# Cached values of a two-layer hybrid decoder: probabilities held stationary, pages moved, four batches in four column groups

## The chip, the cores and the metric

The kernel runs on one core of one Trainium2 chip. The metric is device time in microseconds (us) of one execution, as a median of several.

## The reference, cut to what matters

Two decoder layers run over 520 tokens: one prompt of 512, and a sample group of 8 sequences with one new token each. Each sample sequence has 1024 past tokens in a paged cache, eight pages of 128, and a page table that says which. The part of the mixer on which the change works:

```python
def gather_past(pool, page_table):
    g = pool[page_table]
    return g.reshape((g.shape[0], g.shape[1] * g.shape[2]) + g.shape[3:])
...
(a_q, a_k, a_v, a_iq, a_ik, a_iw, b_q, b_k, b_v, ..., gate) = jnp.split(xn @ w['w_in'], offs, axis=-1)
# A, sparse attention: 4 query heads, 2 key/value heads, top 256 keys by an indexer
p = jax.nn.softmax(logits, axis=-1)
o = jnp.einsum('btjgn,btnjd->btjgd', p, v_sel)
# B, stick-breaking attention, 4 heads
a = jnp.where(mask, jnp.exp(jax.nn.log_sigmoid(z) + after), 0.0)
o = jnp.einsum('bhtl,blhd->bthd', a, v)
...
g = jax.nn.sigmoid(gate.reshape(bsz, t, N_BRANCH, D_MODEL))
merged = g[:, :, 0] * (o_a @ w['w_br_a']) + ... + g[:, :, 3] * (o_d @ w['w_br_d'])
```

A page of cached values holds 384 numbers for each of its 128 tokens: 128 of A (two heads of 64) and 256 of B (four heads of 64). The other two branches are scans over the prompt in chunks of 128 (C, a matrix memory with a norm, and D, a state-space model), four heads each. The gate logits are 4096 columns of the input projection, that is 32 weight tiles of 128 columns. After the mixer come an output projection and a convolutional feed-forward part.

## The kernel before

**Order of a layer.** Weights are loaded as tiles of 128 partitions by 1024 columns. A layer has 29 projection tiles (12, then the cached keys, then 17), 32 gate tiles, then the branch, output, up and down tiles. TensorE, VectorE (DVE), ScalarE (ACT), GpSimd (POOL) and SyncE (SP) each run one program in a fixed written order; semaphores tie them together. A wait such as `pe.wait_ge(*sa_trc.nth(l, 0))` names a signal and the layer.

**Ring and queue.** SP issues nearly all loads, in the order of the list `TILES`. They go into the ring `R` of four slots; a load into a slot waits for `tile_used`, the count of tiles that TensorE is done with. A page of the cache needs its number from the page table `PT` first (`value_load`, line 403), then its own DMA (line 404). SP also stores the gate logits, two halves per tile, with `keep` (line 447).

**Split weights.** A projection or gate tile is multiplied as three matmuls per pass: leading parts `XH` and `WH`, rests `XL` and `WL`. ACT makes `WH` (line 1003, `split`), for the gate tiles POOL makes `WL` (line 1714, `split_rest`). There are two buffers of each, so tile q+2 is split when tile q has been multiplied.

**Gate filling.** The 32 gate tiles are used as filling between other work. The generator `gates(l)` (line 582) yields after each unit of three matmuls of 260 columns; a tile has 16 units, and `fill(upto)` on TensorE runs units until `upto` are done. ACT's `drain(upto)` copies finished halves out of the banks (line 1021) and starts the split of tile q+2; POOL's `follow(upto)` starts the rest. Tables say how far each place fills: `PRE` (seven places before the scans), `LOOP` (eight scan steps), `IN_T` (four places in each of the four attention blocks).

**Places around the change.** After the last projection come, in this order: the transposing of A's sample probabilities (lines 680 and 682); 12 transposes to token-major, `TO_TM` (line 695), each a chunk of four; cumulative sums of the gate logarithms (line 706) and a transpose of rows; the sample group's recurrent state in eight diagonals of 8 rows, which POOL builds and TensorE broadcasts; then eight scan steps v (0 to 3 for C, 4 to 7 for D); then four attention blocks t of the prompt. In a scan step TensorE broadcasts a row (line 758), makes scores (line 776), multiplies cached values, and runs the numerator (line 779); ACT makes decays (line 1166), POOL a diagonal mask (line 1708) and state weights (line 1770), DVE products. After steps 1 and 3 DVE divides (line 1585).

**Cached values.** The probabilities of all sample batches stand in `PA`, a view of `QB`: 256 columns of A, then 256 of B, 32 for each page position. `cached_values(l, b)` (lines 557 and 562) is called once per scan step, for one of the eight batches. Each of its pages is held stationary in three pieces of 128 columns, and the moving operand is 4 columns of probabilities for A, and 2 for each pair of heads of B:

```python
mm(PS[:, 7, 448 + 4 * b:448 + 4 * b + 4], slot(l, n)[:, v0:v0 + 128],
   PA[:, 32 * j + 4 * b:32 * j + 4 * b + 4], start=j == 0, stop=j == 7, ...)
```

These are 192 matmuls a layer, in full fp32 precision. The result is already laid out by feature; nine DVE operations after the scans add it to `OS` and copy it to the branch inputs (signal `sa_out`), for which TensorE waits in the first attention block. The pages lie in the same ring as the gate tiles, interleaved by the list `MIX`: four slots of two pages for each batch.

## Time and profile before

| | |
|---|---|
| median of 3 runs | 2830.28 us (2822.64 to 2831.82) |
| the profiled execution: its time, its span | 2841.91 us, 2839.8 us |
| its mean granted TensorE clock | 0.895 |
| TensorE busy with matmuls | 2540.2 us, 89% |
| DVE, ACT, POOL busy | 1285.4, 1013.4, 348.1 us |
| TensorE's share of the chain that ended last | 31%, DVE 4%, ACT 1% |
| matmuls of gate filling (line 582) | 3072, about 900 us |

A busy TensorE need not be at full speed: the granted clock tells how fast it ran, as a share of 2.4 GHz, and 0.5 is the lower of its two levels. Matmuls overlap each other, so that busy times of single matmuls add up to more than the time they span. The other engines have much slack on average, so what they cost is seen only where TensorE waits for them. The name PEld is the weight load of TensorE, and SPq and ACTq are DMAs issued by SyncE and ScalarE.

### The profile page before, as it was taken

To read this page: it belongs to the slowest core of one execution; us is meant where nothing else is said; L and a number is where in the kernel's file an instruction comes from. 1 tells how busy PE (TensorE), PEld (TensorE's weight loads), DVE (VectorE), ACT (ScalarE), POOL (GpSimd) and SP (SyncE) were. 2 spreads that over 40 slices of the span, in tenths; PEclk is the share of its full clock that TensorE was granted. 3 is DMA by queue.
4 is the path that set the end of the run, shared out by engine and by line. 5 is a ranking of instruction groups with operands and counts; after the bars stand their busy time and mean duration, and the time that the engine had idled before them with its cause. 6 is when DMAs were issued, how large, how long until landed. Compare 5 with 4: busy or idle time off the path is not lost. (4 is left out here: it accounts for less than half of the span.)

```text
span 2839.8 us, 41630 instructions
## 1 busy us (share of the span) xinstructions
PE 2540.2 (89%) x16456; PEld 2175.6 (77%) x16456; DVE 1285.4 (45%) x2047; ACT 1013.4 (36%) x1526; POOL 348.1 (12%) x390
## 2 busy tenths in 40 slices
PE   6999679989999889999888997899899997999996
PEld 5659657767887789999885686477687776999895
DVE  3329341223556465662342383422234565666623
ACT  3123431224444345552230225222244433555521
POOL 0014232112320000000000132311222100000000
PEclk9999766769999899999999997676799998999998
DMA  3362112232326122222314422122322251222221
GB/s 151 111 201 90 58 47 77 77 100 68 89 75 196 60 67 91 97 91 82 103 60 148 156 75 68 58 68 83 92 79 89 84 172 52 83 97 90 88 84 60
DMA packets 111827, 264.00 MB, mean 93 GB/s; under 512 B 13458, under 2 KB 47250, under 8 KB 110738
## 3 DMA queue, kind: packets, MB, share of 16 engines
q1 hardware_dynamic: 99074, 238.25, 26.4%
q10 hardware_dynamic: 12560, 23.11, 2.4%
q8 instruction: 130, 2.13, 0.3%
q14 instruction: 63, 0.52, 0.1%
HBM read 233.71 MB, written 27.59 MB: 92 GB/s over the span
## 5 line engine op out<-in xcount | busy, mean ns | idle before, releaser
L497 PE MATMUL PS<-XH,WH 128*128 128x260 f32 x2592 | 540.2, 290 | 47.9 <-DVE XL L1315 36.3
L1003 ACT ACTIVATE WH<-R 128x1024 fp32r<-128x1024 f32 x270 | 286.0, 1059 | 780.5 <-PE PS L497 564.9
L497 PE MATMUL PS<-XL,WH 128*128 128x260 f32 x2592 | 529.2, 286 | 4.3 <-issue 2.8
L497 PE MATMUL PS<-XH,WL 128*128 128x260 f32 x2592 | 528.1, 285 | 0.0
L1339 DVE TENSOR_TENSOR WL<-R,WH 128x1024 fp32r<-128x1024 f32 x176 | 215.7, 1226 | 555.9 <-ACT WH L1003 555.6
L497 PEld LDWEIGHTS PS<-XH,WH 128*128 128x128 f32 x2592 | 408.6, 193 | 56.7 <-issue 43.7
L497 PEld LDWEIGHTS PS<-XL,WH 128*128 128x128 f32 x2592 | 406.3, 192 | 4.7 <-issue 4.7
L497 PEld LDWEIGHTS PS<-XH,WL 128*128 128x128 f32 x2592 | 405.7, 192 | 0.0
L582 PE MATMUL PS<-XH,WH 128*128 128x260 f32 x1024 | 304.8, 298 | 16.5 <-ACT RB L1021 16.3
L1714 POOL TENSOR_TENSOR WL<-R,WH 128x1024 fp32r<-128x1024 f32 x94 | 223.3, 2376 | 730.8 <-ACT WH L1003 729.9
L582 PE MATMUL PS<-XL,WH 128*128 128x260 f32 x1024 | 298.3, 291 | 0.0
L582 PE MATMUL PS<-XH,WL 128*128 128x260 f32 x1024 | 297.0, 290 | 0.0
L582 PEld LDWEIGHTS PS<-XH,WH 128*128 128x128 f32 x1024 | 202.4, 198 | 29.9 <-issue 22.2
L582 PEld LDWEIGHTS PS<-XH,WL 128*128 128x128 f32 x1024 | 202.1, 197 | 0.0
L582 PEld LDWEIGHTS PS<-XL,WH 128*128 128x128 f32 x1024 | 202.0, 197 | 0.0
L497 PE MATMUL PS<-FR,WH 128*128 128x260 f32 x1024 | 190.8, 289 | 8.9 <-issue 8.9
L497 PEld LDWEIGHTS PS<-FR,WH 128*128 128x128 f32 x1024 | 154.4, 195 | 9.7 <-issue 9.7
L1318 DVE SCALAR_TENSOR_TENSOR S<-S,V 128x510 f32<-128x510 f32 (+1 forms) x176 | 132.1, 751 | 44.9 <-ACT S L1282 41.8
L1021 ACT ACTIVATE RB<-PS 128x260 f32<-128x260 f32 x128 | 49.6, 387 | 246.8 <-PE PS L582 144.7
L915 PE MATMUL PS<-F,R 128*128 128x260 f32 x512 | 119.4, 388 | 4.5 <-DVE F L1315 3.1
L915 PEld LDWEIGHTS PS<-F,R 128*128 128x128 f32 x512 | 94.4, 190 | 29.1 <-DVE F L1315 9.8
L562 PE MATMUL PS<-QB,R 128*128 128x2 f32 x512 | 113.0, 325 | 0.0
(311 smaller groups left out, 3398.9 us busy)
## 6 DMA issues: line engine op xcount, KB each, us to landing
R<-w_up SPq DMA_DIRECT2D x88, 512.0 KB, 3.3
R<-w_gate SPq DMA_DIRECT2D x64, 512.0 KB, 3.7
R<-w_proj SPq DMA_DIRECT2D x58, 512.0 KB, 3.3
R<-v_c SPq DMA_DIRECT2D x128, 192.0 KB, 2.4
R<-w_down SPq DMA_DIRECT2D x44, 512.0 KB, 3.2
R<-k_c SPq DMA_DIRECT2D x72, 256.0 KB, 3.3
GATES<-RB SPq DMA_DIRECT2D x128, 130.0 KB, 3.7
S<-GATES SPq DMA_DIRECT2D x64, 260.0 KB, 2.7
```

The lines of the kernel that those rows point to most:

```text
L497: i = mm(PS[:, bank + a, 0:HALF], p[:, w, k * 128:(k + 1) * 128], x[:, a * HALF:(a + 1) * HALF], start=first and p is WH and x is hi, stop ...
L562: ins = mm(PS[:, 7, o:o + 2], slot(l, n)[:, v0 + 128 + 128 * c:v0 + 256 + 128 * c], PA[:, 256 + 32 * j + 4 * b + 2 * c:256 + 32 * j + 4 * ...
L582: i = mm(PS[:, 1 + 2 * a, 0:HALF], p[:, half(l, m), k * 128:(k + 1) * 128], x[:, k, a * HALF:(a + 1) * HALF], start=k == 0 and p is WH and ...
L915: ins = mm(PS[:, 4 + 2 * (q % 2) + a, 0:HALF], slot(l, nb)[:, 256 * br + 128 * k:256 * br + 128 * k + 128], F[:, o + k, a * HALF:(a + 1) * ...
L1003: do(A(WH[:, half(l, m), :], slot(l, SPLIT[m]), ACT.Copy), w_hi)
L1021: do(A(RB[:, HALF * a:HALF * (a + 1)], PS[:, 1 + 2 * a, 0:HALF], ACT.Copy), g_out)
L1318: do(v_.scalar_tensor_tensor(out, a, sc, b, o0, o1), s)
L1339: v_.tensor_tensor(WL[:, half(l, m), :], slot(l, SPLIT[m]), WH[:, half(l, m), :].bitcast(f32), ALU.subtract).then_inc(w_lo.sem, 1)
L1714: g_.tensor_tensor(WL[:, half(l, m), :], slot(l, SPLIT[m]), WH[:, half(l, m), :].bitcast(f32), ALU.subtract).then_inc(w_lo_p.sem, 1)
```

## The change

**Cached values.** Now 8 columns of probabilities are stationary, A's four and B's four of one batch side by side (`PA` is now a view with 8 columns for each batch and page position), and a whole page of 384 columns moves. Four batches are multiplied in one call, a quad: their results go to partitions 0, 32, 64 and 96 of one bank, which are four column groups of TensorE. A layer has 16 quads of four matmuls, eight for the first four batches (bank 0) and eight for the last four (bank 2). As every matmul adds to its bank (`start=False`), one matmul of 384 columns with zeros clears each bank first. A finished bank is copied by ACT (`values_out`) and turned to feature-major by three small matmuls (`by_feature`).

**Buffers.** The pages have left the ring. Two buffers of four pages each, `QUAD`, lie in parts of `S` and `TM` that are free at that time. Each page is still its own DMA with its number from `PT`, all on SP, four for each quad; quad k waits until quad k-2 has been used.

**Place.** Quads 0 and 1 stand before the token-major transposes, and two more follow each of the first seven chunks. The DVE operations, 18 instead of nine since each half is done apart, move in front of the state products, and TensorE waits for them before `r_tr`, not in the attention blocks.

**Filling.** The tables are new: 144 units up to the end of the token-major transposes where there were 48; 192 before the diagonals (96), four after each of the eight diagonals, eight after each scan step (16 after every second one), and 10 to 26 at each place of the attention blocks instead of 12 to 42. After the last scan step 288 units are done where it was 160. Tile q+2 is always split as soon as tile q is finished, by ACT in `drain` and by POOL in `follow`; the loop `IN_LOOP`, by which both split the next tile in a scan step ahead of the filling, is gone.

**ACT.** The exponential of A's sample probabilities stands after the last projection copy instead of inside the loop over them, and TensorE waits for the last two projection copies before it fills.

```diff
...
-PRE = [0, 32, 48, 64, 72, 80, 96]
-LOOP = [96 + STEPS * (v // 2 + 1) for v in range(8)]
...
+LAST, PAST_P = 16, 24
+IN_TM = [36, 48, 60, 72, 84, 96, 108, 112, 120, 128, 136, 144]
+CUM, ROWS, SEL, DOTS = 160, 176, 184, 192
+IN_R = [DOTS + 4 * (s + 1) for s in range(8)]
+LOOP = [IN_R[-1] + 8 * (v + 1) for v in range(8)]
+IN_T = [[14, 10, 12, 10], [14, 10, 18, 12], [14, 10, 22, 14], [14, 10, 26, 14]]
...
+QUADS_AT = [PAST_P, PAST_P] + [IN_TM[i] for i in range(7) for _ in range(2)]
+LOAD_QUADS = [[k for k in range(NQ) if (QUADS_AT[k - 2] // STEPS + RING - 1 if k >= 2 else 1) == q] for q in range(NG)]
...
@@ sync engine
+                def cached_values(k):
+
+                    s, j = divmod(k, PAGES)
+                    if k == 0:
+                        sp.wait_ge(*sb_a.nth(l, 0))
+                    elif k >= 2:
+                        sp.wait_ge(*quad_used.nth(l, k - 2))
+                    for g in range(4):
+                        sp.dma_start(QUAD[k % 2][:, g, :],
+                                     v_c[l, bass.ds(page(sp, PAGES * (4 * s + g) + j), 1)].rearrange("o p c -> (o p) c")
+                                     ).then_inc(quad_full[k % 2].sem, 16)
+                for q in range(NG):
+                    tile(l, AT["gate", q], w_gate[l, q], 1024)
+                    if q >= RING:
+                        keep(q - RING)
+                    for k in LOAD_QUADS[q]:
+                        cached_values(k)
...
@@ tensor engine
+            def cached_values(l, k):
+
+                s, j = divmod(k, PAGES)
+                pe.wait_ge(quad_full[k % 2].sem, 64 * (NQ // 2 * l + k // 2 + 1))
+                for g in range(4):
+                    ins = mm(PS[32 * g:32 * g + 8, 2 * s, 0:V_REC], PA[:, PAGES * j + 4 * s + g, :], QUAD[k % 2][:, g, :],
+                             start=False, stop=j == PAGES - 1, skip_group_check=True)
+                finish(ins, quad_used)
...
+                for c in (NPROJ - 2, NPROJ - 1):
+                    pe.wait_ge(*proj_out.nth(l, c))
+                fill(LAST)
...
+                for s in range(2):
+                    mm(PS[:, 2 * s, 0:V_REC], K[0:1, C_SEL + 128:C_SEL + 256], K[0:1, 0:V_REC], start=True, stop=False,
+                       skip_group_check=True)
+                fill(PAST_P)
                 pe.wait_ge(*sa_trc.nth(l, 0))
                 pe.wait_ge(*sa_own.nth(l, 0))
+                cached_values(l, 0)
+                cached_values(l, 1)
...
+                    fill(IN_TM[i])
+                    if i < 7:
+                        cached_values(l, 2 * i + 2)
+                        cached_values(l, 2 * i + 3)
+                    if i in (4, 9):
+                        by_feature(l, i // 5)
...
                     finish(ins, r_bc)
+                    fill(IN_R[s])
...
@@ scalar engine
-                        if a:
-                            for nxt in SPLIT_NEXT[q]:
-                                split(l, NPROJ + nxt)
+                        if a and q + 2 < NG:
+                            split(l, NPROJ + q + 2)
...
-                    for q in IN_LOOP[v]:
-                        split(l, NPROJ + q)
...
@@ gpsimd engine
+                    follow(IN_R[s])
...
-                    for q in IN_LOOP[v]:
-                        split_rest(l, NPROJ + q)
                     follow(LOOP[v])
```

Three places of the resulting order follow. In the rows, L is the line, xN a repetition, and the names in brackets are signals waited for.

SP, the start of the gate tiles, in the kernel before (`w_gate` is a gate tile, `GATES` the store of two halves, `v_c` a page of cached values with the table read of `PT` ahead of it):

```order
L424 DMA R<-w_gate 128x1024 [waits tile_used] x5
L447 DMA GATES<-RB 128x260 [waits gate_logits_copied] x2
L424 DMA R<-w_gate 128x1024 [waits tile_used]
L447 DMA GATES<-RB 128x260 [waits gate_logits_copied] x2
L403 TENSOR_LOAD PT [waits tile_used]
L403 ISA x2
L404 ISA
L404 DMA R<-v_c 128x384
...
L404 DMA R<-v_c 128x384
L447 DMA GATES<-RB 128x260 [waits gate_logits_copied] x2
L403 TENSOR_LOAD PT [waits tile_used]
```

The same place after:

```order
L433 DMA R<-w_gate 128x1024 [waits tile_used] x2
L405 TENSOR_LOAD PT [waits sample_b_weights]
L405 ISA x2
L465 ISA
L465 DMA S<-v_c 128x384
...
L465 DMA TM<-v_c 128x384
L433 DMA R<-w_gate 128x1024 [waits tile_used] x3
L454 DMA GATES<-RB 128x260 [waits gate_logits_copied] x2
L405 TENSOR_LOAD PT [waits value_pages_used]
L405 ISA x2
L465 ISA
L465 DMA S<-v_c 128x384
```

The pages came after six gate tiles, and between each two of them stood stores of gate halves. Now the first eight stand after two tiles, the next ones after three more, and eight pages, of two quads, stand between neighbouring tiles or groups of tiles.

TensorE, between the last projection and the first gate filling, before (680 and 682 transpose the probabilities, 695 is the token-major transpose of `F`, 582 the gate filling):

```order
L680 MATMUL PS<-K,S 128x32 [waits sample_a_probs]
L680 MATMUL PS<-K,S 128x32 x7
L682 MATMUL PS<-DG,K 128x32
L695 MATMUL PS<-K,F 128x128 [waits rope_done,projection_copied,sample_a_own_value,sample_a_probs_copied]
L695 MATMUL PS<-K,F 128x128 x3
L695 MATMUL PS<-K,F 128x128 [waits projection_copied]
L695 MATMUL PS<-K,F 128x128 x3
...
L695 MATMUL PS<-K,F 128x128 [waits projection_copied,token_major_ready]
L695 MATMUL PS<-K,F 128x128 x3
L582 MATMUL PS<-XH,WH 128x260 [waits weight_rest_part_ready_by_pool,weight_leading_part_ready]
L582 MATMUL PS<-XL,WH 128x260
```

The same place after (702 and 704 answer to 680 and 682, 707 is the clearing of the banks, 601 the filling, 570 a quad, 723 the token-major transpose):

```order
L702 MATMUL PS<-K,S 128x32 [waits sample_a_probs]
L702 MATMUL PS<-K,S 128x32 x7
L704 MATMUL PS<-DG,K 128x32
L707 MATMUL PS<-K 128x384 x2
L601 MATMUL PS<-XH,WH 128x260 [waits gate_logits_copied,weight_rest_part_ready_by_pool,weight_leading_part_ready]
...
L570 MATMUL PS<-S,QB 8x384 [waits value_pages0_loaded,sample_a_own_value,sample_a_probs_copied]
L570 MATMUL PS<-S,QB 8x384 x3
L570 MATMUL PS<-TM,QB 8x384 [waits value_pages1_loaded]
L570 MATMUL PS<-TM,QB 8x384 x3
L723 MATMUL PS<-K,F 128x128 [waits projection_copied,rope_done]
L723 MATMUL PS<-K,F 128x128 x3
L601 MATMUL PS<-XH,WH 128x260 [waits gate_logits_copied]
```

Before, eight chunks of transposes followed each other without filling; now two quads stand ahead of the first chunk, and 12 units and two quads behind it.

ACT, scan steps 1 and 2, before (1164 and 1166 are the decays, 1003 the split of a gate tile, 1021 the copy of a half, 1177 and 1179 the norm of C):

```order
L1166 ACTIVATE F<-F 128x1280 [waits decay_exponent_ready]
L1003 ACTIVATE WH<-R 128x1024 [waits tile_used,slot3_full,decay_exp_done]
L1021 ACTIVATE RB<-PS 128x260 [waits gate_half0_stored,gate_first_half_done,weight_leading_part_ready]
L1021 ACTIVATE RB<-PS 128x260 [waits gate_half1_stored,tile_used,gate_logits_copied]
L1164 ACTIVATE F<-PS,SMT 128x512 [waits numerator_done,row_broadcast,gate_logits_copied]
...
L1166 ACTIVATE F<-F 128x1280 [waits decay_exponent_ready]
L1177 ACTIVATE S<-PS 128x512 [waits numerator_done,decay_exp_done]
L1179 ACTIVATE S<-S 128x520 [waits c_h_ready,c_denominator_abs]
```

The same place after (1201 and 1203 are the decays, 1031 the split, 1049 the copy, 1212 and 1214 the norm):

```order
L1203 ACTIVATE F<-F 128x1280 [waits decay_exponent_ready]
L1049 ACTIVATE RB<-PS 128x260 [waits gate_half0_stored,gate_first_half_done,decay_exp_done]
L1201 ACTIVATE F<-PS,SMT 128x512 [waits numerator_done,row_broadcast,gate_logits_copied]
...
L1203 ACTIVATE F<-F 128x1280 [waits decay_exponent_ready]
L1212 ACTIVATE S<-PS 128x512 [waits numerator_done,decay_exp_done]
L1214 ACTIVATE S<-S 128x520 [waits c_h_ready,c_denominator_abs]
L1049 ACTIVATE RB<-PS 128x260 [waits gate_half1_stored,tile_used,c_squares_ready]
L1031 ACTIVATE WH<-R 128x1024 [waits tile_used,slot1_full,gate_logits_copied]
L1201 ACTIVATE F<-PS,SMT 128x512 [waits numerator_done,row_broadcast,weight_leading_part_ready]
```

The split stood ahead of both copies, and the step's decays behind them; now it stands behind the second copy, which itself has moved behind the norm of C.

## Rows read from the trace of the kernel before

**Rows 1.** Page, part 1: busy time, share of the span, instructions.

```profile
PE 2540.2 (89%) x16456; PEld 2175.6 (77%) x16456; DVE 1285.4 (45%) x2047; ACT 1013.4 (36%) x1526; POOL 348.1 (12%) x390
```

**Rows 2.** Windows, layer 0: length, busy PE, PEld, DVE, ACT, POOL; PEclk; DMA share; GB/s.

```profile
302.70:351.60 48.90, 28.70 (x204) 27.13 (x203) 19.14 (x45) 30.48 (x50) 9.47 (x4) 0.82 0.22 73
351.60:407.40 55.80, 45.98 (x212) 31.68 (x212) 29.12 (x51) 15.53 (x26) 18.84 (x13) 0.74 0.17 55
407.40:611.10 203.70, 191.41 (x860) 142.43 (x860) 39.33 (x58) 47.25 (x67) 43.44 (x102) 0.68 0.27 81
611.10:857.60 246.50, 226.17 (x1425) 185.68 (x1425) 114.59 (x280) 105.57 (x189) 57.95 (x56) 0.93 0.27 79
```

**Rows 3.** Windows, PE, probabilities' tile only, scans of both layers.

```profile
sum 420.00, PE 143.22; mean PE 71.61
```

**Rows 4.** Timeline, PE: start, us, instruction, count, [idle before]; first and last pages.

```profile
421.44 0.59 PE L557 MATMUL PS<-QB,R 128*128 128x4 f32 x2
...
422.74 0.57 PE L557 MATMUL PS<-QB,R 128*128 128x4 f32 x2
...
449.12 0.39 PE L557 MATMUL PS<-QB,R 128*128 128x4 f32 x2
...
449.81 0.36 PE L557 MATMUL PS<-QB,R 128*128 128x4 f32 x2
```

**Rows 5.** Windows, PE, line 582 only: length, busy, clock, DMA; 16 units each.

```profile
353.20:361.50 8.30, 8.22 (x48) 0.69 0.00 0
439.50:445.60 6.10, 6.04 (x48) 1.00 0.00 0
```

**Rows 6.** Timeline, PE, cached keys of layer 0.

```profile
144.26 0.61 PE L637 MATMUL PS<-R,QI 64*32 64x256 f32 x2
144.80 0.40 PE L639 MATMUL PS<-R,QA 128*32 128x256 f32 x1
144.81 0.40 PE L647 MATMUL PS<-R,QB 128*32 128x256 f32 x1
...
145.79 0.62 PE L637 MATMUL PS<-R,QI 64*32 64x256 f32 x2
```

**Rows 7.** Timeline, SP, layer 0; last line: page, part 6.

```profile
342.74 1.45 SPq L404 DMA_DIRECT2D R<-v_c  x2
344.23 0.91 SPq L447 DMA_DIRECT2D GATES<-RB  x2
...
R<-v_c SPq DMA_DIRECT2D x128, 192.0 KB, 2.4
```

**Rows 8.** Timeline, splits, POOL's weights and DVE's reciprocal, scans of layer 0.

```profile
452.07 1.37 POOL L1708 TENSOR_SCALAR_AFFINE_SELECT F<-F 128x128 f32<-128x128 f32 x4 [16.04 <-ACT F L1166]
...
454.52 2.05 POOL L1770 TENSOR_SCALAR S<-TM,U 128x64 f32<-128x64 f32 x4
...
468.39 3.35 DVE L1585 RECIPROCAL S<-S 128x512 f32<-128x512 f32 x1
...
581.88 1.06 ACT L1003 ACTIVATE WH<-R 128x1024 fp32r<-128x1024 f32 x1 [1.91 <-DMA R<-w_gate]
...
583.08 2.35 POOL L1714 TENSOR_TENSOR WL<-R,WH 128x1024 fp32r<-128x1024 f32 x1 [14.15 <-ACT WH L1003]
```

**Rows 9.** Waits, PE, whole kernel: waited for, total us, times, longest.

```profile
PE PS L706 <- DVE SMT L1315: 17.4, 2, 8.7
```

**Rows 10.** Timeline, ACT, sigmoid and SiLU ahead of the scans, layer 0.

```profile
384.10 1.28 ACT L1153 ACT_TABLE_LOAD   x1
...
388.01 1.30 ACT L1155 ACTIVATE F<-F 128x520 f32<-128x520 f32 x2
```

**Rows 11.** Timeline, last attention block of layer 0.

```profile
802.43 1.84 ACT L1208 ACTIVATE F<-PS 128x512 f32<-128x512 f32 x4 [1.56 <-PE PS L849]
...
810.57 1.37 POOL L1708 TENSOR_SCALAR_AFFINE_SELECT F<-F 128x128 f32<-128x128 f32 x4 [8.17 <-DVE F L1318]
...
838.59 0.15 DVE L1321 TENSOR_SCALAR MX<-MX 128x1 f32<-128x1 f32 x1
```

More of the change, by code:

```diff
@@ L214, in trunk_kernel @@
         slot_full = [sig(f"slot{i}_full", 0) for i in range(RING)]
-        tile_used = sig("tile_used", NPROJ + 2 * NU + 40 + 8 + 44 + 22)
+        tile_used = sig("tile_used", NPROJ + NU + 40 + 8 + 44 + 22)
+        quad_full = [sig(f"value_pages{i}_loaded", 0) for i in range(2)]
+        quad_used = sig("value_pages_used", NQ)
         xt_ready = sig("normalised_ready", 16)
@@ L436, in _ @@
                     if not by_act(u):
-                        cached(sp, l, AT["K", u], u, K_REC, k_c)
+                        cached_keys(sp, l, u)
                 for c in range(CUT, NPROJ):
                     tile(l, proj(c), w_proj[l, c], 1024)
-                def keep(n):
-                    if TILES[n][0] == "gate":
-                        q = TILES[n][1]
-                        for a in range(2):
-                            sp.wait_ge(*g_out.nth(l, 2 * q + a))
-                            sp.dma_start(GATES[l, q, :, HALF * a:HALF * (a + 1)],
-                                         RB[:, HALF * a:HALF * (a + 1)]).then_inc(g_stored[a].sem, 16)
@@ L449, in _, with keep @@
-                for kind, i in MIX:
-                    n = AT[kind, i]
-                    if kind == "V":
-                        cached(sp, l, n, i, V_REC, v_c)
-                    else:
-                        tile(l, n, w_gate[l, i], 1024)
-                    keep(n - RING)
+                def keep(q):
+                    for a in range(2):
+                        sp.wait_ge(*g_out.nth(l, 2 * q + a))
+                        sp.dma_start(GATES[l, q, :, HALF * a:HALF * (a + 1)],
+                                     RB[:, HALF * a:HALF * (a + 1)]).then_inc(g_stored[a].sem, 16)
@@ L456, in _ @@
+                for q in range(NG):
[4 more added lines that the diff above has]
+                        cached_values(k)
                 for d in range(2):
                     tile(l, AT["br", d], w_br[l, d], 1024)
-                    keep(AT["br", d] - RING)
-                for n in range(AT["br", 2] - RING, AT["br", 0]):
-                    keep(n)
+                for q in range(NG - RING, NG):
+                    keep(q)
@@ L709, in _ @@
                 finish(ins, sm_cum)
-                fill(PRE[3])
+                fill(CUM)
                 pe.wait_ge(*sm_rt.nth(l, 0))
@@ L714, in _ @@
                 finish(ins, sm_tr)
-                fill(PRE[4])
+                fill(ROWS)
                 pe.wait_ge(*xbc_ready.nth(l, 5))
@@ L722, in _ @@
                 finish(ins, r_sel)
-                fill(PRE[5])
+                fill(SEL)
                 pe.wait_ge(*r_prod.nth(l, 0))
@@ L730, in _ @@
                 finish(ins, r_tr)
-                fill(PRE[6])
+                fill(DOTS)
                 for s in range(8):
@@ L1049, in _ @@
                             if by_act(u):
-                                cached(act, l, AT["K", u], u, K_REC, k_c)
+                                cached_keys(act, l, u)
                         split(l, CUT)
@@ L1109, in _ @@
                     token_major(c)
-                token_major(7)
-                drain(PRE[1])
-                for i in range(8, len(TO_TM)):
+                for i in range(7, len(TO_TM)):
                     token_major(i)
-                drain(PRE[2])
                 act.wait_ge(*sm_v.nth(l, 0))
@@ L1149, in _ @@
                 do(A(S[0:8, 3, 0:512], PS[0:8, 2, :], ACT.Copy), r_trc)
-                drain(PRE[6])
+                drain(DOTS)
+                for s in range(8):
+                    drain(IN_R[s])
                 for c in range(2):
@@ L1492, in _ @@
                 tt(MR, SROW[0:4, :], PS[64:68, 5, :], ALU.add, sm_g)
+                for s in range(2):
+                    dve.wait_ge(*sv_out.nth(l, s))
+                    o = OS[:, 16 * s:16 * s + 16]
+                    tt(o, o, PS[:, 2 * s, 384:400], ALU.add)
+                    for h in range(4):
+                        r0 = 64 * (h // 2)
+                        do(v_.tensor_copy(F[r0:r0 + 64, AQ + h % 2, NPR + 4 * s:NPR + 4 * s + 4], o[r0:r0 + 64, h:16:4]))
+                    for h in range(4):
+                        r0, c = 64 * (h % 2), h // 2
+                        do(v_.tensor_copy(F[r0:r0 + 64, BQ + c, NPR + 4 * s:NPR + 4 * s + 4],
+                                          PS[r0:r0 + 64, 2 * s, 400 + 8 * c + h % 2:408 + 8 * c:2]),
+                           sa_out if s and h == 3 else dve_own)
                 dve.wait_ge(*tm_ready.nth(l, 9))
@@ L1733, in follow @@
                     while STEPS * (behind[0] + 1) <= upto:
-                        for nxt in SPLIT_NEXT[behind[0]]:
-                            split_rest(l, NPROJ + nxt)
+                        if behind[0] + 2 < NG:
+                            split_rest(l, NPROJ + behind[0] + 2)
                         behind[0] += 1
-                follow(PRE[4])
+                follow(DOTS)
                 pool.wait_ge(*r_trc.nth(l, 0))
```

111 lines of the change are left out of this document (48 added, 63 removed).

## The prediction

> **What bounds the kernel now.** I read the page's table of engines, then the busy time by stage, then each engine's instructions inside the stages. TensorE is busy 89% of the span [rows 1], so what counts is its own work, its waits and its clock. In layer 0 the touched stretch runs from 302.7 to 857.6 us, and I call its four parts turn, rows, scans and attention: 48.9, 55.8, 203.7 and 246.5 us, with granted clocks of 0.82, 0.74, 0.68 and 0.93 of 2.4 GHz [rows 2]. Layer 1 has the same four parts shifted by about 1407 us (the matmuls of the cached values take 143.22 us in the two windows, 71.6 in each) [rows 3], so I work out one layer and double it. The 71.4 us of layer 0's cached values lie wholly in the scans and wholly on TensorE's path. A page (three matmuls, six passes) takes 1.30 us at the start of one batch and 0.69 us at the start of another [rows 4], a factor of nearly two: these matmuls move 2 or 4 columns each, and the clock falls to 1.2 GHz while they run. A gate tile is 16 units; 16 units take 6.04 us at clock 1.00 and 8.22 us after a long wait at 0.69 [rows 5]. So a unit is 0.375 us, and a long wait costs about 2.2 us more in lost clock.
>
> **Turn, +59.8 us a layer.** It holds 144 units where it held 48. The start: gate halves share banks with the last two projections, so TensorE waits for ACT's split and copy, 1.06 us [rows 8] and an estimated 0.8; 16 units 6.0; transposed probabilities 0.8 and the two zeroing matmuls 1.3 (estimates from passes, below); 8 units 3.0. That is 13.0. Then seven steps of one chunk transposed, 12 units and two quads. **The quads on TensorE:** the change has 64 matmuls of 384 moving columns a layer. Cached keys show the nearest row: fp32 matmuls of 256 columns start a pass every 0.24 us, and two in neighbouring column groups start 0.01 us apart, so that eight passes take 1.53 us instead of about 1.9 [rows 6]. By columns a pass of 384 is 0.35 us. If four groups run side by side a quad is 0.75 us, one after the other 2.7; I take 0.75 because the one pair that could overlap did so completely. A step then is 0.5 + 12 x 0.375 + 2 x 0.75 = 6.5 us of TensorE. **The quads on SP:** every page is its own DMA with its number read from a table, and two such in a row span 1.45 us, the second ending 1.1 after the first; a pair of gate stores takes 0.91, and a page lands 2.4 us after its issue [rows 7]. There are two buffers, so from quad 2 on all 56 pages are issued inside these steps, each group of four behind the use of the quad two before: 56 x 1.1 = 61.6, five gate tiles with their stores 5 x 1.3 = 6.5, the last landing and its use 3.2, the first use 0.8: 72.1 us, against 7 x 6.5 + 0.8 = 46 if SP were free. So TensorE waits some 26 us here, and what is queued behind the waiting SP, gate tiles and stores, is needed two tiles later and stays covered. After that five chunks with 36 units take 16.3. Last, ACT still has to evacuate and split the tile just finished before it starts the gate logarithms, whose table loads cause today's wait of 8.7 us a layer (17.4 for two) [rows 9]; I keep 7.4. 13.0 + 72.1 + 16.3 + 7.4 = 108.8, against 48.9.
>
> One row and one rule disagree here. By the row, four pages keep SP busy 4.4 us, while a page lands 2.4 us after its issue [rows 7]: the issue is the larger part. The Trainium skill ("DMA: Bandwidth & Descriptors", Issuing engines are not separate DMA queues) says that the issue is usually small beside the DMA itself. By that rule the 26 us would go; by the row they stay, and the sum goes by the row.
>
> **Rows, +17.8.** 32 more units, 12.0. GpSimd splits tile q+2 only when tile q is finished, and it now stands ahead of the first and of the fifth of the eight diagonals: from the end of the fill, ACT's copy and split 1.5, POOL's split 2.35 [rows 8], the diagonal 2.2 (an estimate): two waits of 6.3. DVE takes over the 18 small outputs of the cached values (3.4 us), hidden beside units of filling. The part runs at 0.74 now; its busy time at full clock would be some 12 us shorter. Units between the broadcasts should win back 7 of it (bounds 0 and 12). 12.0 + 12.7 - 7 = 17.8.
>
> **Scans, -57.7.** Gone are 71.4, and 3.0 of filling that now lies behind the last numerator. But the cached values also covered a chain. Before, ACT split the next gate tile ahead of the filling; now it does so behind it, and POOL's split stands in front of the next scan step's diagonal and state weights. After step 1 and step 3: numerator, DVE's maximum, reciprocal of 3.35 us and product [rows 8], ACT's square, copy and split, POOL's split 2.35, then its weights 4.5 (452.07 to 456.57) [rows 8], DVE's first product: 16.3 us in sum, of which TensorE fills 6: waits of 10.2 twice, where 3.5 stand now. After step 5: 7.3. Steps 3 and 5 wait for the norm's root that six fewer us of filling cover: 3.0 and 2.7. Step 0: ACT's sigmoid and SiLU with two table loads, 5.2 us (384.10 to 389.31) [rows 10], move behind the last fill and delay the first decay: with a faster start for TensorE, 6.3 more. Waits in sum +32.4. Clock: without the cached matmuls TensorE's other 120 us would take some 93 at full clock, so 27 are lost now; four long waits lose about 2.9 each afterwards, hence -15.7 (bounds 0 and -27). -71.4 - 3.0 + 32.4 - 15.7 = -57.7.
>
> **Attention, -24.8.** 128 units fewer, -48.0. They hid others' work: from the logits to the masked softplus ACT, DVE and POOL need 9.5 us (802.43 to 811.94) [rows 11], and 1 us plus 14 units cover 6.3; the next mask needs 4.8 (an estimate) behind 10 units, 3.75; in the last block DVE's selection ends at 838.74 [rows 11], later than TensorE would come. Less the copy stalls that stand there now this makes 4.1, 2.8, 2.3 and 5.3, in sum 14.5. Waits of 3.5 us are long enough to lose the clock (the clock after a wait, above): 8.7. The removed wait for the cached output costs nothing now, since its eight DVE copies hide behind the state store.
>
> **Sum.** 59.8 + 17.8 - 57.7 - 24.8 = -4.9 a layer, -9.8 in all. The profiled execution took 2841.9 us (span 2839.8), so 2832; it lies 11.6 above the median of 2830.3, so I forecast 2821. Work moved is large, the net is small, and each of the four parts could be off by 10.
>
> **Rivals.**
> 1. *The clock comes back for good* (faster). For it: the low clock sits where the cached values are, 0.68 [rows 2]. Against: waits come in their place. If the waits cost no clock, rows win 5 more, scans 11, attention 9: 25 a layer, about 2771. 0.19.
> 2. *SP's issue hides* (faster). Without the number read from the table an issue is shorter: a pair of gate stores takes 0.91 us, 0.45 each [rows 7]. If a page is issued at that pace, because SP reads the next number while the DMA before is still being issued, the 56 pages take 25 us and TensorE's 46 set the end: 26 us a layer less, 2769. This is what the rule of the Trainium skill named above amounts to. Against it is the pair of pages in the row, which shows no such overlap. 0.05.
> 3. *The clock does not come back* (slower). Filling is cut into 4 and 8 units between matmuls of 8 rows or few columns, with waits of 6 to 10 us between; then rows and scans stay near 1.2 GHz. The 7 and 15.7 us of gain vanish: +22.7 a layer, 2866. It decides from about a third of that, 7 us a layer. 0.25.
> 4. *The four groups do not run side by side*, so the change does not do what it says. TensorE needs 5.0 + 5.4 = 10.4 a step against SP's 68.1 / 7 = 9.7, so most of it hides behind SP: 7 x 0.7 = 5 a layer, 2831. 0.13.
> The forecast has 0.38.
>
> **How the numbers follow.** Within 0.3%, about what a measurement can tell from no change, means 2822 to 2839. The forecast lies on the edge: of its 0.38 about 0.19 are faster, 0.15 the same, 0.04 slower. Rivals 1 and 2 are faster (0.24), rival 3 is slower (0.25), rival 4 splits 0.02, 0.06 and 0.05. Faster 0.45, same 0.21, slower 0.34. The range goes to both clock cases with a little beyond them for errors of the waits: 2765 to 2878; the forecast's own is 2809 to 2833.
>
> **What would show it.** Quad matmuls in fours with starts 0.01 us apart (else rival 4). TensorE waiting on page loads 20 to 30 us a layer, and SP issuing one page per 1.1 us without a pause (else rival 2, and the turn is over-priced). Waits of about 10 us ahead of scan steps 2 and 4 and 7 ahead of step 6, released by DVE behind POOL's weights; two of 6 in rows. Waits of 3.5 at the start of each attention block. Granted clock in the scans near 0.85 (rival 1 above 0.9, rival 3 below 0.75). The forecast falls if ACT's or SP's order adds a wait that I missed, or if ACT's chain ahead of the scans is not where I put it.

## The result, and the profile after

The changed kernel takes 2889.6 us (median of 4 runs, 2878.6 to 2901.5) against 2830.7 for the kernel before: 1.0215 times as long, 95% interval 1.0164 to 1.0266. I had forecast 2821 with a range of 2765 to 2878. It is slower, and above the range. One execution of the kernel with halved pages (experiment 8) took 3913 us at a mean granted clock of 0.55 and is left out of the ratios.

The profiled execution has a span of 2898.2 us. The page's table of engines, to be read beside [rows 1]:

```profile
PE 2468.3 (85%) x15976; PEld 2067.0 (71%) x15976; DVE 1288.4 (44%) x2065; ACT 1015.4 (35%) x1530; POOL 347.1 (12%) x390
```

TensorE is busy 72 us less than before and the span is 58 us longer, so 130 us more are waits or other idle time. Where they lie is told by the four stages of layer 0. The busy time by window of the changed kernel, cut at the same instructions as [rows 2] (length, then busy time of PE, PEld, DVE, ACT and POOL, granted clock, DMA share, GB/s):

```profile
301.30:419.80 118.50, 85.49 (x636) 70.21 (x635) 24.30 (x48) 43.72 (x72) 23.80 (x10) 0.84 0.56 165
419.80:504.60 84.80, 67.97 (x309) 50.64 (x309) 31.29 (x70) 14.76 (x26) 25.23 (x16) 0.68 0.16 50
504.60:655.50 150.90, 110.08 (x454) 66.11 (x453) 39.99 (x57) 50.25 (x71) 38.73 (x100) 0.75 0.07 22
655.50:884.00 228.50, 191.24 (x1065) 145.75 (x1065) 110.57 (x271) 92.28 (x167) 41.37 (x49) 0.90 0.21 62
```

| part of layer 0 | before, us | after, us | change | forecast | idle time of TensorE, before and after |
|---|---|---|---|---|---|
| turn | 48.9 | 118.5 | +69.6 | +59.8 | 20.2, 33.0 |
| rows | 55.8 | 84.8 | +29.0 | +17.8 | 9.8, 16.8 |
| scans | 203.7 | 150.9 | -52.8 | -57.7 | 12.3, 40.8 |
| attention | 246.5 | 228.5 | -18.0 | -24.8 | 20.3, 37.3 |
| sum | 554.9 | 582.7 | +27.8 | -4.9 | 62.6, 127.9 |

Twice 27.8 is 55.6 of the 59.6 us by which the two profiled executions differ. All four parts missed in the same direction.

TensorE's waits in the whole kernel (waited for, us in total, times, longest), those that bear on the change:

```profile
PE PS L811 <- DVE F L1350: 37.4, 8, 9.0
PE PS L570 <- DMA TM<-v_c: 36.7, 11, 4.9
...
PE PS L808 <- DVE F L1350: 34.7, 6, 9.0
PE PS L601 <- ACT RB L1049: 24.8, 8, 5.0
PE PS L896 <- POOL F L1744: 20.8, 8, 3.6
PE PS L736 <- DVE SMT L1350: 14.8, 2, 7.4
...
PE PS L773 <- POOL F L1785: 12.6, 2, 6.3
...
PE PS L777 <- POOL F L1791: 12.1, 2, 6.1
...
PE PS L570 <- DMA S<-v_c: 10.4, 8, 2.3
```

Lines 808 and 811 are the scores of a scan step, 570 the quads, 601 the filling, 896 the cumulative sums of attention, 773 and 777 the diagonals' broadcasts. Line 736 is the cumulative sum ahead of the rows, whose wait is not new (17.4 before) and took the 7.4 us a layer that were forecast. The waits are the ones that the prediction named, in place and nearly in length: 23.6 us a layer for pages (26 forecast), 6.3 and 6.1 in the rows (6.3 each), 8.95 ahead of scan steps 2 and 4 (10.2), 6.9 ahead of step 6 (7.3). What had been priced too low is the clock behind them. The eight diagonals have four broadcasts of 64 columns (line 773) and four of 128 (line 777), each with a slice of four units of filling behind it. TensorE's timeline (start, us, instruction, [idle before]) shows some of the broadcasts,

```profile
457.15 1.97 PE L773 MATMUL PS<-F,K 8*64 8x512 f32 x4 [6.31 <-POOL F L1785]
461.95 1.97 PE L773 MATMUL PS<-F,K 8*64 8x512 f32 x4
466.75 1.07 PE L773 MATMUL PS<-F,K 8*64 8x512 f32 x4
...
478.14 3.78 PE L777 MATMUL PS<-F,K 8*128 8x512 f32 x4 [6.06 <-POOL F L1791]
484.75 3.78 PE L777 MATMUL PS<-F,K 8*128 8x512 f32 x4
```

and the windows of TensorE alone (length, PE busy, granted clock) show the clock in the first half, which changes in its middle, and in the second:

```profile
457.10:466.70 9.60, 9.55 (x32) 0.50 0.01 2
466.80:472.10 5.30, 5.29 (x33) 1.00 0.00 0
478.10:504.50 26.40, 26.36 (x64) 0.50 0.00 0
```

Six of the eight slices ran at clock 0.50 and took 2.97 us each; the third and the fourth ran at 1.00 and took 1.7. In an unbroken stretch four units take 1.5 [rows 5]. After the last slice the clock stays at 0.50 until 528.0, 23 us into the scans.

### The profile page after: what moved, and what is told of

It reads as the page before. It is cut to its first block and busy times, and to the rows that moved or that the text cites. A ratio compares the mean times of both kernels' runs of the same rounds, so it can differ in the third digit from the quotient of the medians.

```text
span 2898.2 us, 40698 instructions
## 1 busy us (share of the span) xinstructions
PE 2468.3 (85%) x15976; PEld 2067.0 (71%) x15976; DVE 1288.4 (44%) x2065; ACT 1015.4 (35%) x1530; POOL 347.1 (12%) x390
## 5 line engine op out<-in xcount | busy, mean ns | idle before, releaser
L514 PE MATMUL PS<-XH,WH 128*128 128x260 f32 x2592 | 538.1, 289 | 45.3 <-DVE XL L1350 36.3
L514 PE MATMUL PS<-XL,WH 128*128 128x260 f32 x2592 | 528.0, 285 | 5.6 <-issue 5.6
L514 PE MATMUL PS<-XH,WL 128*128 128x260 f32 x2592 | 526.3, 285 | 0.0
L514 PEld LDWEIGHTS PS<-XH,WH 128*128 128x128 f32 x2592 | 407.0, 192 | 54.0 <-issue 41.2
L514 PEld LDWEIGHTS PS<-XL,WH 128*128 128x128 f32 x2592 | 405.4, 191 | 6.0 <-issue 6.0
L514 PEld LDWEIGHTS PS<-XH,WL 128*128 128x128 f32 x2592 | 404.1, 191 | 0.0
L601 PE MATMUL PS<-XH,WH 128*128 128x260 f32 x1024 | 321.7, 314 | 28.6 <-ACT RB L1049 24.8
L601 PE MATMUL PS<-XL,WH 128*128 128x260 f32 x1024 | 309.5, 302 | 0.0
L601 PE MATMUL PS<-XH,WL 128*128 128x260 f32 x1024 | 308.4, 301 | 0.0
L601 PEld LDWEIGHTS PS<-XH,WH 128*128 128x128 f32 x1024 | 214.2, 209 | 68.7 <-issue 56.4
L601 PEld LDWEIGHTS PS<-XL,WH 128*128 128x128 f32 x1024 | 214.2, 209 | 0.0
L601 PEld LDWEIGHTS PS<-XH,WL 128*128 128x128 f32 x1024 | 214.0, 209 | 0.0
L1353 DVE SCALAR_TENSOR_TENSOR S<-F,V,S 128x520 f32<-128x520 f32 (+3 forms) x72 | 62.4, 867 | 76.4 <-ACT S L1140 74.3
```

Of the source, the lines that this page charges most:

```text
L514: i = mm(PS[:, bank + a, 0:HALF], p[:, w, k * 128:(k + 1) * 128], x[:, a * HALF:(a + 1) * HALF], start=first and p is WH and x is hi, stop ...
L601: i = mm(PS[:, 1 + 2 * a, 0:HALF], p[:, half(l, m), k * 128:(k + 1) * 128], x[:, k, a * HALF:(a + 1) * HALF], start=k == 0 and p is WH and ...
L1353: do(v_.scalar_tensor_tensor(out, a, sc, b, o0, o1), s)
```

## The experiments

Each is the changed kernel with the edit shown. Stages are those of layer 0, cut as above, and each is read from one execution. Where a stage's program was left alone, its length still varied: the turn from 115.4 to 118.5 us, the rows from 84.8 to 88.3, the attention from 219.3 to 228.5.

**1. The slices of filling between the diagonals, filled ahead of them.**

```diff
-CUM, ROWS, SEL, DOTS = 160, 176, 184, 192
-IN_R = [DOTS + 4 * (s + 1) for s in range(8)]
+CUM, ROWS, SEL, DOTS = 160, 176, 184, 224
+IN_R = [DOTS] * 8
```

> The changed kernel with one edit: the 32 units of gate filling that stand in slices of four between the eight diagonals' broadcasts are all filled ahead of the first broadcast. Theory A (in slices the filling runs at the lower clock, and the second POOL split makes a second wait): 12 us of clock and the second wait of 6.1 us go, 18 a layer: about 2854 us. Theory B (the part is slow whatever stands in it, since the wait ahead of the broadcasts lowers the clock for the filling too): only the second wait goes, 6 a layer: about 2877 us.

Measured: 2851.3 us, 1.0085 of the kernel before (1.0055 to 1.0115). That is 38 us less than the changed kernel, as theory A had it. But by stage neither theory holds, and the total agrees with A partly by luck: the rows fell by 8.9 us a layer (84.8 to 75.9) where A had 18, the scans by 4.6 and the attention by 2.5. In the rows TensorE's busy time fell by 7.0 us. The filling, now ahead of the wait for the first broadcast, ran at full clock; the broadcasts themselves still ran at 0.50, and so did the first 18 us of the scans. The second wait went as expected, but the idle time of the rows fell by only 1.9 us, since shorter waits came for ACT, for POOL (14.2 us for line 773 in the whole kernel, 12.6 before) and, ahead of the first scan step, 1.8 for DVE.

**2. POOL's split of the next gate tile one scan step later, and two diagonals later.**

```diff
-                follow(DOTS)
+                follow(SEL)
...
-                    follow(IN_R[s])
+                    follow(IN_R[s - 2] if s >= 2 else (SEL, DOTS)[s])
...
-                    follow(LOOP[v])
+                    follow(LOOP[v - 1] if v else IN_R[-1])
+                follow(LOOP[-1])
```

> The changed kernel with one edit: POOL splits the next gate tile one scan step (and two diagonals) later, behind the mask and the weights of the step that follows, not ahead of them. Theory A (POOL's split in front of the next step holds TensorE): the two waits of 6.2 us in the rows nearly go, the two of 8.95 ahead of steps 2 and 4 fall to the 3.5 of before, the one of 6.9 ahead of step 6 goes: 26 a layer, about 2837 us. Theory B (ACT's copy and split, or DVE's division, end only a little earlier): each of five waits falls by the 2.35 us of POOL's split alone, 12 a layer, about 2866 us.

Measured: 2781.4 us, 0.9851 (0.9804 to 0.9897). Theory A was right in kind, and the effect is twice what it gave: 108 us instead of 52. The windows of rows and scans:

```profile
422.20:485.90 63.70, 57.53 (x308) 45.27 (x309) 32.06 (x69) 14.76 (x26) 25.34 (x16) 0.79 0.21 67
485.90:606.60 120.70, 101.96 (x453) 61.70 (x453) 39.31 (x58) 50.27 (x71) 38.99 (x100) 0.83 0.09 27
```

Beside the windows of the changed kernel: TensorE's idle time fell by 10.6 us in the rows and 22.1 in the scans, and its busy time, with the same instructions, by another 10.4 and 8.1. So each microsecond of wait that was taken away brought more than half a microsecond of clock with it. Between the diagonals the clock came back in one half only (TensorE alone: length, PE busy, granted clock):

```profile
454.90:469.90 15.00, 14.98 (x52) 0.54 0.14 46
469.90:485.90 16.00, 15.93 (x78) 1.00 0.16 49
```

Two broadcasts of its second half:

```profile
475.13 1.98 PE L777 MATMUL PS<-F,K 8*128 8x512 f32 x4
478.68 1.98 PE L777 MATMUL PS<-F,K 8*128 8x512 f32 x4
```

In the second half there is no wait any more, and a broadcast of line 777 with its slice takes 3.54 us, against 6.61 in the changed kernel. In the first half a wait of 1.6 us for POOL is left of the 6.3. The clock behind it is low for three slices, not for fewer than in the changed kernel, where it was two. So the length of a wait alone does not tell what it costs, and the runs do not show what else decides it.

Why POOL's place matters is seen in POOL's timeline of the changed kernel ahead of scan step 2, where split (1750), mask (1744) and weights (1807) follow each other, and TensorE waits 8.95 us until 561.1:

```profile
553.33 2.34 POOL L1750 TENSOR_TENSOR WL<-R,WH 128x1024 fp32r<-128x1024 f32 x1 [27.85 <-ACT WH L1031]
555.74 1.37 POOL L1744 TENSOR_SCALAR_AFFINE_SELECT F<-F 128x128 f32<-128x128 f32 x4
```

POOL had been idle 27.85 us, since its split waits for ACT's, which waits for the end of a tile of filling. The decays for its mask were ready at 540.5, 15.2 us before the mask began. Of these only 2.4 are the split itself; the other 12.8 are POOL's wait in front of it.

**3. Both places apart: late in the scan steps only** (the last hunk of the diff above).

> The changed kernel with POOL's split late in the scan steps only; between the diagonals it stays ahead. Theory A (each wait costs its own length and the clock just behind it): the rows keep their 84.8 us, the scans lose the 30 a layer that they lost with both places late, about 2829 us. Theory B (the low clock that the waits in the rows leave behind reaches into the scans): the scans lose only 20 to 24 a layer, 2841 us or more.

Measured: 2824.7 us, 0.9981 (0.9959 to 1.0002). Theory A. The rows stayed slow and the scans fell by 33:

```profile
419.00:507.30 88.30, 71.44 (x309) 52.33 (x309) 31.29 (x70) 14.76 (x26) 25.24 (x16) 0.65 0.15 48
507.30:625.10 117.80, 101.53 (x454) 60.37 (x454) 40.04 (x57) 50.25 (x71) 38.77 (x100) 0.85 0.09 28
```

So the split in the scan steps costs 65 us in both layers, and the one between the diagonals the other 43. That the two parts can be told apart does not mean that the low clock ends with the rows. It goes on until 528 us in the changed kernel and until 532 here, 23 and 25 us into the scans. In experiment 2 too it is at 0.52 from 489.9 to 510.8, in the first 25 us of the scans, which have waits of their own for ACT and DVE, so that nothing was to be gained there.

**4. Pages loaded once.** From the third quad on no pages are loaded; the values of the sample group are left wrong by it.

```diff
                     for k in LOAD_QUADS[q]:
-                        cached_values(k)
+                        if k < 2:
+                            cached_values(k)
...
-                pe.wait_ge(quad_full[k % 2].sem, 64 * (NQ // 2 * l + k // 2 + 1))
+                pe.wait_ge(quad_full[k % 2].sem, 64 * (l + 1))
```

> The changed kernel without the loads of pages from the third quad on: all quads multiply what the first two loaded, so 56 of 64 page loads a layer are left out and the values of the sample group are not those of the reference. Theory A (SP's issue of pages is what TensorE waits for in the turn): the 23.6 us of waits for pages go and with them some 10 us of lowered clock, 34 a layer: about 2822 us. Theory B (behind the pages stands another wait, ACT's copies of the chunks and of the gate halves): 10 a layer or less, 2870 us or more.

Measured: 2823.6 us, 0.9976 (0.9953 to 0.9998). Theory A: the turn falls by 36 us, of which TensorE's busy time is 12.3, the clock again (0.84 to 0.98):

```profile
304.70:387.20 82.50, 73.16 (x636) 62.45 (x635) 24.36 (x48) 43.77 (x72) 23.83 (x10) 0.98 0.35 103
```

**5. Who bounds the turn: half of the page loads on another queue.** These and the following have POOL's late split as well (0.985), but for the first of experiment 7. In the first, ACT loads every second quad: `load_quad(act, l, 2 * i + 5)` behind each chunk's copy, and SP only the even ones.

> POOL's late split (2781 us measured) and, in addition, half of the page loads, those of every second quad, issued by ACT instead of SP. Theory A (SP's issue is the bound of the turn): SP's step of 10.7 us shrinks to about 7, ACT's grows to about 9 (4.5 of copies and 4.5 of issue), so the turn loses 7 x 1.7 = 12 us of waits and some of the lowered clock: 15 a layer, about 2750 us. Theory B (the time from issue to landing is the bound, since a quad's pages can only be loaded when the one two before it is used): nothing, 2781 us. Theory C (ACT, now with waits for the quads in its order, is late with its copies): slower than 2781.

Measured: 2767.1 us, 0.9791 (0.9740 to 0.9842), the turn 110.5 us against 117.2: half of what A gave. The intervals of the two kernels overlap, so by time alone this is not told from the late split without it. With POOL as the second issuer:

> The same with POOL instead of ACT as the second issuer; POOL has only 24 of 118 us of work in the turn. Theory A: SP's part alone bounds the step then, at 7 us against TensorE's 6.5: the turn comes near the 82.5 us that it took with the pages loaded once, 30 us a layer less, about 2721 us. Theory B (landing time is the bound): 2781 us. If an issue takes POOL much longer than SP's 0.9 us a page, POOL becomes the bound and the time goes up.

Measured: 2777.6 us, 0.9819 (0.9777 to 0.9861), which the intervals don't tell from 0.985; the turn even grew to 121.6 us. A of this run was wrong. SP's timeline in the run with ACT, and the quad that it loads for:

```profile
326.25 3.63 SPq L415 DMA_DIRECT2D S<-v_c  x4
```

```profile
333.63 0.83 PE L572 MATMUL PS<-S,QB 128*8 128x384 f32 x8 [2.60 <-DMA S<-v_c]
```

The buffer was free at 325.4 (end of the quad before); the first page was issued 0.85 us later, the last at 329.9, and the quad began 3.7 us after that. That is 8.2 us from use to use, and 9 with the quad itself, against 6.5 us of TensorE's work at full clock. A second queue does not shorten this cycle; it even lengthened the landing. A page's median time from issue to landing was 2.6 us in the changed kernel and 3.2 and 3.5 here:

```profile
TM<-v_c SPq DMA_DIRECT2D x64, 192.0 KB, 2.6
```

```profile
TM<-v_c ACTq DMA_DIRECT2D x64, 192.0 KB, 3.5
S<-v_c SPq DMA_DIRECT2D x64, 192.0 KB, 3.2
```

POOL issued a page every 1.15 us and often came late to its turn.

**6. ACT's sigmoid and SiLU ahead of its copies between the diagonals** (with the late split):

```diff
                 drain(DOTS)
+                for c in range(2):
+                    do(A(F[:, CO + c, :], F[:, CO + c, :], ACT.Sigmoid), c_sg)
+                for c in range(2):
+                    do(A(F[:, DZ + c, :], F[:, DZ + c, :], ACT.Silu), d_sl)
                 for s in range(8):
                     drain(IN_R[s])
```

> POOL's late split and, in addition, ACT's sigmoid and SiLU with their two table loads (5.2 us) ahead of its copies between the diagonals, not behind them. Theory A (ACT's order ahead of the first scan step adds 5.2 us to TensorE's wait there): the waits of 6.2 and 6.0 us at the first scan step fall by 5.2 together, about 2771 us. Theory B (another input of the first step is as late, or the copies of gate halves are now late): 2781 us or more.

Measured: 2764.4 us, 0.9767 (0.9725 to 0.9809), an interval that just overlaps that of the late split. A by stage: the wait of 6.2 us for ACT is gone, that of 6.0 for DVE stays, and the scans fell by 4.3 us. The attention of this run is 6.8 us shorter too, though its program is the same; in all runs with the same attention it lay between 219.3 and 228.5 us, with clocks of 0.93 to 0.89, so part of the gain in time may be chance.

**7. The old filling tables**, alone and with the late split. The edit puts `PRE`, `LOOP` and `IN_T` back by their numbers.

> The changed kernel with the filling tables of the kernel before (48 units in the turn, 96 before the diagonals, none between them, 16 after every second scan step, 12 to 42 at the places of attention), all else as changed. Theory A (the new places of the filling cost more than the cached values give back): turn 97, rows 61, scans 147, attention 247 us, sum 552 a layer against 583 measured: about 2828 us. Theory B (the tables matter little, the pages and the new waits of the quads do): within 10 of the changed kernel, 2880 us.

Measured: 2882.0 us, 1.0204 (1.0171 to 1.0236), not told apart from the changed kernel: B by the number. By stage it is not so simple: 105.0, 64.1, 153.8 and 248.3 us. The old tables take 34 us off turn and rows and give 23 back to scans and attention. This is read from two executions that differ by 23 us, where the medians differ by 8.

> POOL's late split together with the filling tables of the kernel before. With the tables alone put back the time fell by only 8 us. Theory A (the split's place hid what the tables do; the turn of 105 us and the attention of 248 stay, rows 57, scans 125): 535 a layer, about 2796 us, so the new tables are worth 15 us once the split is late. Theory B (the tables bring nothing): 2781 us or less.

Measured: 2825.8 us, 1.0000 (0.9983 to 1.0017), 30 above A and 45 above B, so neither. With the split late the new tables are worth 1.5%, and with it early nothing that can be measured. By stage (105.5, 61.7, 127.2, 254.0) the new tables cost 12 us in the turn for 96 more units, which are 36 us of work at full clock. TensorE's idle time in the turn is 17 us shorter with them (31.7 against 48.5), and the rest of the difference is clock, 0.85 against 0.62.

**8. Together.** Late split, early sigmoid and every second quad by ACT:

> Late split, early sigmoid and every second quad issued by ACT: three edits that gave 108, 17 and 14 us in steps. If they act in different places they add up: about 2750 us. If ACT's page issue takes back what the early sigmoid gave, 2764 us or more.

Measured: 2747.7 us, 0.9737 (0.9677 to 0.9797); the three add up, as far as so wide an interval can tell. With each quad's pages halved between SP and ACT instead:

> POOL's late split and the early sigmoid (2764 us measured) and, in addition, every quad's four pages issued half by SP and half by ACT. With whole quads on either queue the cycle of a buffer stayed: use, 0.85 us to the first issue, 3.6 of issue, 3.7 to landing, about 9 us for every two quads against TensorE's 6.5. Theory A (that cycle is the bound): issue falls to 1.8, the cycle to 7.2, and the turn from 117 to about 97 us: 20 a layer, about 2724 us. Theory B (ACT's and SP's other work between the quads is the bound, copies of chunks, gate halves and their stores): no better than 2764 us.

Measured: 0.9716 of the kernel before (0.9641 to 0.9790), some 2751 us. A had 2724, and neither the run before it nor experiment 6 is told from it by the intervals. The turn:

```profile
303.70:406.30 102.60, 78.22 (x634) 64.51 (x634) 22.33 (x48) 43.73 (x72) 23.77 (x10) 0.94 0.61 191
```

From 116.9 to 102.6 us, where A gave 97. But the same turn took 107.6 us in the next run, and with whole quads on two queues it took 110.5 and 109.1. The waits for pages in it were 15.1 and 15.4 us with halved pages, against 16.3 and 18.7 with whole quads on two queues and 23.7 in the changed kernel. So the two queues took away a fifth to a third of these waits, halving the pages added a few microseconds at most, and that the cycle of the buffers bounds the turn is not shown. The landing grew again, and may have taken back part of what the issue gave:

```profile
S<-v_c ACTq DMA_DIRECT2D x32, 192.0 KB, 3.2
TM<-v_c ACTq DMA_DIRECT2D x32, 192.0 KB, 3.4
S<-v_c SPq DMA_DIRECT2D x32, 192.0 KB, 3.1
TM<-v_c SPq DMA_DIRECT2D x32, 192.0 KB, 3.7
```

Last, on top of it, the units between the diagonals moved to attention (`IN_R = [DOTS] * 8`, and 22 for 14 at each block's first place):

> Late split, early sigmoid, halved pages (0.972 of the kernel before, about 2751 us), and the 32 units between the diagonals moved to the first place of the four attention blocks, 8 more in each, where TensorE waits 3.4, 1.6, 2.2 and 3.2 us for POOL's mask. Theory A (filling is free only where somebody else is late): the eight broadcasts take the 24 us of the kernel before instead of 31, the units add 12 us to attention and take away the 10.4 us of waits: 5 to 6 a layer less, about 2740 us. Theory B (the mask is then later by as much, or the broadcasts without filling run at the lower clock and wait for POOL): 2751 us or more.

Measured: 2740.2 us, 0.9674 (0.9652 to 0.9697), the fastest of all: 93 us less than the kernel before. From the run before it the intervals don't tell it. Its rows took 60.4 us instead of the 54 of A. The broadcasts without filling wait 5.3 us a layer for POOL, and the clock of the rows fell from 0.83 to 0.67, both as B had it. But in attention the mask's wait (here line 897, before 896) is nearly gone, and attention took 221.6 us with 32 more units, against 222.9:

```profile
PE PS L897 <- POOL F L1752: 1.7, 4, 0.5
```

## Why the prediction was wrong

- **The quads on TensorE, right.** A quad was forecast at 0.75 us: its eight passes lie within 0.83 us, and the next quad starts 0.65 after the first. Rival 4 is out.

```profile
314.13 0.83 PE L570 MATMUL PS<-S,QB 128*8 128x384 f32 x8
314.78 0.83 PE L570 MATMUL PS<-TM,QB 128*8 128x384 f32 x8
```

- **The waits, right as a whole.** In rows, scans and attention the forecast had 12.7, 32.4 and 14.5 us of added idle time; measured were 7.0, 28.5 and 17.0.
- **The clock, the step that failed.** For the rows I took a gain of 7 us, "units between the broadcasts should win back 7". The 32 units there cost 21 us instead of 12 (six slices of 2.97 and two of 1.7) and won back nothing; the busy time of the part grew by 22.0 us where 12 less 7 were forecast, 17 too few. In the scans I took -15.7, of which 8.8 did not come (busy time -81.3 instead of -90.1), in attention 4.3 were missing. I priced a long wait by its own length and 2.2 to 2.9 us of clock behind it, read from filling that ran on without a break [rows 5], and in the rows I put no price at all on the clock behind the two new waits. There short slices, broadcasts of 8 rows and the next waits follow, and behind the second wait the clock stayed at 1.2 GHz for 50 us, through the waits of 3.8 and 5.9 us of the first scan step. In the scans 46.8 us of TensorE's busy time lay at clock 0.50. By an estimate half of that, 23 us, is lost clock, against 12 for my four waits. It lay at their start and behind waits of 2.4 and 2.6 us too, not only behind the four long ones. That the waits take this clock is shown by taking them away (experiment 2): 18.5 us of busy time a layer went with 32.7 us of waits. This is rival 3, which had a chance of 0.25 and a price of 22.7 a layer for rows and scans; measured are 25.8 there, and 30 with attention. Its sign, a clock in the scans below 0.75, is met only at the edge (0.75); in the rows the clock was 0.68, lower than the 0.74 of before.
- **SP in the turn, the mechanism right, its size not.** A step of two quads took SP 11.2 us and not 9.7. SP's issue at the start of the turn in the changed kernel:

```profile
315.72 3.64 SPq L465 DMA_DIRECT2D S<-v_c  x4
320.47 3.60 SPq L465 DMA_DIRECT2D TM<-v_c  x4
324.11 0.43 SPq L433 DMA_DIRECT2D R<-w_gate  x1
324.59 0.91 SPq L454 DMA_DIRECT2D GATES<-RB  x2
326.65 3.63 SPq L465 DMA_DIRECT2D S<-v_c  x4
```

A page costs 0.91 us, less than the 1.1 taken, but ahead of each group of four stands a pause, in most cases of 0.75 to 1.15 us, even where its buffer was already free. I had read the price of a page in mid-queue [rows 7] and left out the start of a group. From this first group to the last one of the `S` buffer, at 382.67, six steps take 11.2 us on average, 9.3 to 13.2; in two of them SP also stood still for 1.4 and 2.4 us ahead of a gate tile, which waits for a slot of the ring. Seven times the 1.5 too few are 10 us, about what the turn missed by (9.8). The landing was as forecast: a quad that waited for its pages began 2.2 to 3.5 us behind the last issue, in the median 2.4.
- **The rule of the skill.** The Trainium skill ("DMA: Bandwidth & Descriptors", Issuing engines are not separate DMA queues) would have made rival 2: it did not happen, the pages' waits were 23.6 us. The issue of four pages takes 3.6 us here, while a page lands 2.6 us after its issue, so the issue of a group is not small beside the DMA; that of one page, 0.91 us, is a third of it. The same section says that spreading the issue over several engines saves only the time of the issue. Experiments 5 and 8 agree: the landing did not get shorter, it grew from 2.6 to between 3.1 and 3.7 us.
- **Attention, 6.8 off.** 2.5 are waits, 4.3 the clock. The clock part is no more than what the same program varies by from run to run.
- **The range** was made case by case, each with the other terms as forecast. Here clock and turn missed together: +30.1 and +9.8 a layer, attention's waits +2.5, and the waits in rows and scans were 9.6 shorter than forecast, in sum +32.8. No single case reached 2890; rival 3 (2866) with the turn's 20 us in both layers comes to 2886.
- **The cause below all this** was in the prediction, as a price of 10.2 us for a wait: that POOL's split moved in front of the mask. I took it as one term among many. The five waits that it lengthens were worth 26 us a layer by my own count (the expectation of experiment 2) and 54 by the result, since their clock goes with them. Undoing it turns 1.0215 into 0.9851, so it is enough by itself to turn the sign.

## What to carry to other kernels

An operation that waits for the end of filling must not stand in an in-order engine ahead of one that the critical chain needs soon: delay it to the last place where its result is still in time. Price a new wait with the clock that it takes from the work behind it, here 0.4 us for each us of wait in the scans and 1.0 in the rows (experiment 2). In the rows only short slices of work stand behind the waits, and moving them ahead of the first wait gave back 7.0 us of busy time (experiment 1). When a load sits between two uses of its buffer, add up the pause ahead of the issue, the issue and the landing, and compare the sum with the work between the uses. Don't take the landing over from a kernel with one queue: with pages on two queues it was longer, and a second queue gave less than the sum promised.

## What the runs showed of the hardware

- Four broadcasts of 8 rows, each with a slice of 12 matmuls of 260 columns behind it, ran at clock 0.50 for 26.4 us behind a wait of 6.06 us; the same instructions without the wait ran at 1.00, each pair in 3.54 us instead of 6.61. But behind a wait of 1.6 us three slices ran at 0.50, and behind one of 6.3 only two.
- A page load issued by POOL takes 0.54 us with pauses of 0.6 between them, 1.15 us a page, against 0.91 on SP, and in that kernel it gained nothing.
- Two queues that issued two pages each at the same time (the halved pages: SP from 318.09, ACT from 318.12) took 1.45 us each for it, no longer than one queue alone [rows 7]. The landing did get longer, in the median 3.1 to 3.7 us a page, against 2.6 with one queue.
